# First mixer: the sums of squares of queries and keys, one tile at a time, between the products of the values' third panel

## The reference

```python
def even_mixer(h, w_in, b_f, g_v, w_s, b_s, g_qn, g_kn, w_out):
    z = h @ w_in
    ...
    q = z[..., o:o + FOX_WIDTH].reshape(B, S, FOX_HEADS, FOX_HEAD_DIM)
    k = z[..., o + FOX_WIDTH:o + 2 * FOX_WIDTH].reshape(B, S, FOX_HEADS, FOX_HEAD_DIM)
    vv = z[..., o + 2 * FOX_WIDTH:o + 3 * FOX_WIDTH].reshape(B, S, FOX_HEADS, FOX_HEAD_DIM)
    log_f = jax.nn.log_sigmoid(f_logit)
    q = rms_norm(q, g_qn)     # mean of squares over the 64 elements of a head
    k = rms_norm(k, g_kn)
    y_a = chunk_gmlp(u, v, g_v, w_s, b_s)
    y_b = forgetting_attention(q, k, vv, log_f).astype(h.dtype)
    return jnp.concatenate([y_a, y_b], axis=-1) @ w_out
```

## Time and profile before

| | us |
|---|---|
| median of 3 runs | 2710.07 |
| lowest, highest | 2708.39, 2711.19 |
| the profiled execution | 2715.63 |
| its span, first to last instruction | 2713.8 |
| mean granted TensorE clock in it | 0.981 |

### The profile page before, as it was taken

The page is one execution under the profiler, slowest core; times in us unless marked ns, Lnnn a source line. Parts: engine busy times, 40 slices in busy tenths (PEclk is TensorE's granted clock), DMA queues, the critical chain, the costliest instruction groups (busy, mean ns, idle before and its releaser), DMA issues. The chain is left out here.

```text
span 2713.8 us, 34008 instructions
## 1 busy us (share of the span) xinstructions
PE 2603.3 (96%) x12132; PEld 2123.3 (78%) x12132; DVE 1429.3 (53%) x2139; ACT 945.1 (35%) x1660; POOL 373.1 (14%) x313
## 2 busy tenths in 40 slices
PE   6988999999999999999998898999999998999999
PEld 5866888877777788888877786788878777788887
DVE  5896444435687544443453565544434656544422
ACT  5454323223466332322334433332222224332321
POOL 2003000011165400012100130200011050300000
PEclk9999999999999999999998998999999998999999
DMA  4201333233200133323321031333223322133322
GB/s 148 78 1 57 99 98 94 72 107 129 82 1 1 57 99 96 96 72 108 107 81 32 23 103 46 91 95 97 83 85 119 93 85 93 57 98 94 96 97 70
DMA packets 61149, 219.82 MB, mean 81 GB/s; under 512 B 7152, under 2 KB 7408, under 8 KB 60672
## 3 DMA queue, kind: packets, MB, share of 16 engines
q1 hardware_dynamic: 58896, 209.15, 25.0%
q0 software_dynamic: 2160, 9.44, 1.0%
HBM read 216.47 MB, written 2.10 MB: 81 GB/s over the span
## 5 line engine op out<-in xcount | busy, mean ns | idle before, releaser
L212 PE MATMUL psum<-xh,wh 128*128 128x512 f32 x1880 | 738.2, 393 | 29.9 <-DVE wl L195 22.8
L214 PE MATMUL psum<-xh,wl 128*128 128x512 f32 x1880 | 734.7, 391 | 0.0
L213 PE MATMUL psum<-xl,wh 128*128 128x512 f32 x1880 | 734.6, 391 | 0.0
L189 ACT ACTIVATE wh<-raw 128x1024 fp32r<-128x1024 f32 x404 | 420.9, 1055 | 784.9 <-PE psum L214 777.2
L195 DVE TENSOR_TENSOR wl<-raw,wh 128x1024 fp32r<-128x1024 f32 x404 | 551.4, 1377 | 130.0 <-ACT wh L189 127.1
L212 PEld LDWEIGHTS psum<-xh,wh 128*128 128x128 f32 x1880 | 354.3, 188 | 106.3 <-issue 24.1
L214 PEld LDWEIGHTS psum<-xh,wl 128*128 128x128 f32 x1880 | 354.0, 188 | 75.2
L213 PEld LDWEIGHTS psum<-xl,wh 128*128 128x128 f32 x1880 | 354.3, 188 | 74.1
L212 PE MATMUL psum<-hidden_high,wh 128*128 128x512 f32 x704 | 276.4, 393 | 4.2 <-DVE wl L195 3.7
L213 PE MATMUL psum<-hidden_low,wh 128*128 128x512 f32 x704 | 274.1, 389 | 0.0
L214 PE MATMUL psum<-hidden_high,wl 128*128 128x512 f32 x704 | 274.0, 389 | 0.0
(11 more groups left out here) (382 smaller groups left out, 3289.0 us busy)
## 6 DMA issues: line engine op xcount, KB each, us to landing
raw<-ffn_in SPq DMA_DIRECT2D x176, 512.0 KB, 3.5
raw<-ffn_out SPq DMA_DIRECT2D x64, 448.0 KB, 4.2
raw<-ffn_out SPq DMA_DIRECT2D x32, 512.0 KB, 3.6
raw<-pw SPq DMA_DIRECT2D x24, 512.0 KB, 3.6
raw<-o_w_hgg SPq DMA_DIRECT2D x12, 512.0 KB, 4.1
raw<-w_q SPq DMA_DIRECT2D x8, 512.0 KB, 3.5
raw<-w_o SPq DMA_DIRECT2D x8, 512.0 KB, 3.5
raw<-e_w_qk SPq DMA_DIRECT2D x8, 512.0 KB, 3.6
```

Of the source, the lines that this page charges most:

```text
L189: self.nc.scalar.activation(self.wh[:, slot, :], self.raw[:, slot, :], ACT.Copy).then_inc(self.weights_high.sem, 1)
L212: nc.tensor.matmul(out, ah, bh, start=start, stop=False)
L213: nc.tensor.matmul(out, ah, bl, start=False, stop=False)
L214: return nc.tensor.matmul(out, al, bh, start=False, stop=stop)
```

## The change

`FoxValues.tensor` no longer takes all sums of squares ahead of panel 2. The sums of one tile become a method, `HeadSums.sum`, and panel 2 calls it after each of its eight groups of three wide matmuls. The last call stands behind the signal that the panel is used. The queues of ScalarE and VectorE are unchanged. The wait of `HeadSums.tensor` on `root` is not made on this path; its value there is 0 (these are the first sums that the program reserves), for which `after` issues no wait.

```diff
-    def panel(self, pe, j):
+    def panel(self, pe, j, between=None):
...
                 mm = three(c.nc, c.psum[:, (self.product0 + i) % RING_BANKS, :], ah[:, k, t], al[:, k, t],
                            c.wh[:, slot, w], c.wl[:, slot, w], k == 0, k == KD - 1)
+                if between and (b, i) != (1, self.tiles - 1):
+                    between(pe, b * self.tiles + i)
         mm.then_inc(c.panels_used.sem, 1)
+        if between:
+            between(pe, 2 * self.tiles - 1)
...
     def tensor(self, pe):
-        c = self.c
         after(pe, self.root, self.r0)
         for t in range(len(self.tiles)):
-            pe.wait_ge(self.squares.sem, self.s0 + t + 1)
-            for i in range(self.nt):
-                mm = pe.matmul(c.psum[:, 7, self.at(t, i)], self.buffers[t][:, i * P:(i + 1) * P], self.mean,
-                               start=True, stop=True, skip_group_check=True)
-            mm.then_inc(self.stat.sem, 1)
+            self.sum(pe, t)
+
+    def sum(self, pe, t):
+        c = self.c
+        pe.wait_ge(self.squares.sem, self.s0 + t + 1)
+        for i in range(self.nt):
+            mm = pe.matmul(c.psum[:, 7, self.at(t, i)], self.buffers[t][:, i * P:(i + 1) * P], self.mean,
+                           start=True, stop=True, skip_group_check=True)
+        mm.then_inc(self.stat.sem, 1)
...
         self.forget_sums.along(pe)
-        self.head_sums.tensor(pe)
-        self.panel(pe, 2)
+        self.panel(pe, 2, between=self.head_sums.sum)
         self.forget_sums.spread(pe)
```

## The result

| | kernel before | changed kernel |
|---|---|---|
| median, us | 2710.55 (16 runs) | 2716.55 (16 runs) |
| lowest to highest, us | 2707.69 to 2716.54 | 2712.28 to 2720.75 |
| the profiled execution, us | 2715.63 | 2712.28 |

The changed kernel is slower: ratio 1.002, with a 95% interval of 1.0013 to 1.0027. No run of it came near the forecast of 2703.9; the fastest is 8 us above. The two profiled executions happen to stand the other way round: that of the changed kernel is the fastest of its 16, that of the kernel before is near the slow end of its range. So the stretch around the change has to be read by itself, and the rest apart from it.

The account below looks back on a forecast made before the run. TensorE, busy 96% of the span, was taken as the bound, with this stretch at half clock. Order -6.5 and later root +0.35 gave -6.15 us: 2710.07 to 2703.9 for the median, range 2701.8 to 2715.6.

Parts of the forecast that it names:

- Rival A: TensorE, panel 2: clock falls early, half speed until into `spread`; +4.6 us (+3 to +6.5), time 2714.7; chance 0.34.
- part (3): ScalarE's root waits for the last sum, delaying split and copy, so TensorE waits once in `spread`; +0.35 us (0 to 1.0).
- the weighing of the mix against two other stretches: Panel 2's mix lies between stretches at 666.0 (clock kept) and 2343.6 (lost), nearer the first; clock stays up: 0.48.
- Part (1): TensorE, sums and panel 2 interleaved at full clock: 1.58 us a group, 12.7 us against 19.19, so -6.5 us.
- the pull-ahead of weight loads: TensorE's sums: if several loads were pulled ahead, 1.6 us instead of 7.2, some 5 us lower; not counted.
- Part (2): TensorE's waits for ScalarE's squares before each tile's sums in panel 2: squares finished long before, cost 0.
- Part (4): VectorE's reciprocal and third low split come about 6 us later, with slack before their readers; cost 0.

Follow-up runs that it names:

- `along` apart: Changed kernel with `along` split into parts of 2, 4, 6 and 8 records between groups of panel 1; 2706.27 us, ratio 0.998 to the kernel before.
- `along` three groups earlier: Changed kernel with `along` whole but put behind the fifth group of panel 1; 2708.78 us, ratio 0.9984 to the kernel before.
- thinner mix: Changed kernel with 4 sum records behind each panel 2 group and each `spread` head, root and reciprocal queued later; 2716.21 us, ratio 1.0006 to the kernel before.
- `along` apart, sums in a block: Kernel before, all 64 sum records ahead of panel 2, with only `along` split between groups of panel 1; 2710.09 us, ratio 0.9995.

## Why the prediction was wrong, point by point

**Rival A is what happened.** It was given 0.34. It named the place (the clock lost by the end of the first group, panel 2 at half pace, `spread` in part), and its price for this stretch was +4.6 us; measured are 38.85 - 34.13 = +4.7. That the two agree so closely is in part luck. The price counts five wide matmuls and about twelve narrow records as done when the clock falls, but in the new order only the eight of the first group can stand ahead of the fifth wide one; the changeovers at half pace are left out; and its own terms give 1427.7 + 19.2 = 1446.9 for the start of `spread`, not 1447.3. The terms measured: `spread` starts 1446.98 - 1422.30 = 24.7 us after `along` does, and before 1444.91 - 1423.57 = 21.3, so 3.3 us later where 2.4 were counted; `spread` itself takes 8.7 us in place of 7.35, so 1.4 more where 1.8 and part (3) were counted.

**The step that failed** is the weighing of the mix against two other stretches. It asked whether three wide matmuls and eight narrow records hold the clock, and answered yes. That was right: `along` apart holds it over all eight groups. But the prediction took that answer for the whole question. `along` was left out of the weighing, although the rival said that it stands directly ahead, and although a row showed the clock lost after 2.2 us of narrow records. The kernel with `along` three groups earlier loses the clock in 2.0 us with no sum near it (behind a pause of 0.20 us). The prediction put the clock at 1.00 through panel 2; it was 0.50 from 1426.0 to 1450.0, and that is 38.85 us in place of the 27.90 that the same instructions take with `along` apart. In all 16 runs of the changed kernel the time speaks for a lost clock: the fastest, 2712.28, is slower than the slowest run with `along` apart, 2709.26 (on another chip). I had read the two different delays of the rows as a sign that executions would part about evenly, and only the thinner mix shows any sign of such parting.

**Part (1), the order at full clock,** was right in its size. With the clock held, a group takes 1.59 us (forecast 1.58), the eight take 12.6 from the first wide matmul of panel 2, at 1424.95, to `spread` (forecast 12.7), and the stretch is 6.2 us shorter (forecast 6.15 with part 3): 6.6 less for sums and panel 2, 0.2 more for the broken-up `along`, 0.1 more for `spread`. Two rows were read a little off: before, the sums take 1437.58 - 1425.72 = 11.86 us and the panel 7.33, not 11.79 and 7.4; the sum of the two is unchanged. The weight loads don't hide: eight records between wide matmuls still take 0.8 us, at full clock. So the pull-ahead of weight loads that the Trainium skill describes in TensorE: Matmul & The Clock Gate, Part 2: What happens when you issue a matmul, does not show for several loads in a row in any trace here.

**Part (2), the waits for squares,** cost nothing: no idle time of TensorE stands ahead of any sum.

**Part (3), the later root,** was put at 0.35 us and is about 0.1. With `along` apart ScalarE reads

```profile
1437.74 0.31 ACT L1185 ACTIVATE fox_rms<-psum,eps 128x64 f32<-128x64 f32 x1 [7.86 <-PE psum L1173]
1437.95 1.05 ACT L189 ACTIVATE wh<-raw 128x1024 fp32r<-128x1024 f32 x1
1438.89 1.33 ACT L2499 ACTIVATE sums<-psum 128x512 f32<-128x512 f32 x2
```

and the first copy starts 1438.89 - 1437.56 = 1.33 us into `spread`, where before it was 1446.14 - 1444.91 = 1.23. The root began 0.18 us into `spread` where 0.25 were counted, and the split began 0.21 us after the root, before the root's 0.31 us were over; the sum had them one behind the other. `spread` takes 7.47 us in place of 7.35, without an idle piece. In the changed kernel itself `spread` runs at half pace at first, and this part is covered: no idle time of TensorE in it.

**Part (4)** cost nothing here. Its twin in the memory attentions did cost: there the reader of the reciprocal comes at once, and the work moved away had been its cover.

**The range** ended at 2715.6 and the median is 2716.55. Rival A's price for the stretch came out right, and its 4.6 us were added to a median; the medians differ by 6.0. Where the other 1.3 us are is open: the two profiled executions differ by more than that outside the stretch. The kernel before, too, has 2710.55 us over 16 runs where the forecast started from 2710.07. The upper bound that I had given the rival itself, +6.5, would have held it.

## What to carry to other kernels

Narrow matmuls between wide ones cost what they cost in a block, at an unchanged clock; what moves the time is which clock the stretch gets. Before interleaving narrow work into dense work, look at what stands directly ahead: a mix may keep the full clock and still be too thin to win it back, so a short unbroken run of narrow records in front of it can turn a gain of 6 us in the stretch into a loss of 5. And where a block of small work is dissolved, ask what it had been covering on the other engines.

## What the runs showed of the hardware

The same work can keep either clock. The mix of three wide matmuls and eight narrow records stayed at 2.4 GHz for all eight groups, 12.6 us, where it began there, and at 1.2 GHz for seven groups, 20.9 us, where it did not. At half clock a group's narrow records stretch from 0.8 to 1.5 us, and so do its wide ones, changeover included, so the same alternation goes on at about half the rate. With half as many narrow records a group the clock stayed down as well, for 20.3 us with part of `spread`.

TensorE has no idle time in either stretch: the clock was lost while it was busy all the time with narrow records and a few wide ones. From the first narrow record of such a stretch to the fall it took 2.0 us (`along` earlier, behind a pause), 2.2, 3.7 (the changed kernel), 3.9 (thinner sums), 4.1 (before) and 4.5 (`along` apart, sums in a block). The Trainium skill, TensorE: Matmul & The Clock Gate, A second HAM failure mode: psum-queue depth-cycling, tells of a clock that goes to and fro, with short idle gaps between groups; here there were no gaps, and it went once and stayed.

And 24 wide matmuls that nothing reads paid for themselves and 5.4 us more, against the changed kernel's stretch.
